# Moving the gated activations of the expert value stage by 64 and 128 bytes within SBUF

## The reference, cut to what matters

```python
def _peer(h, w_q, sub_keys, u_emb, v_emb):
    ...
    def retrieve(args):
        tb, eb, gb = args
        act = jax.nn.gelu(jnp.einsum('tkd,td->tk', u_emb[eb], tb), approximate=False) * gb
        return jnp.einsum('tk,tkd->td', act, v_emb[eb])
...
        x = x + _peer(_rmsnorm(x, norm2_g[l]), peer_w_q[l], peer_sub_keys[l], peer_u[l], peer_v[l])
    return _rmsnorm(x, final_g)
```

## The kernel before, in words

| stage, matmul line | moving operand | stationary operand | stationary minus moving, modulo 256 |
|---|---|---|---|
| value stage, L3329 | `v_gated` 64 | `gated_gelu` 64 | 0 |
| `u_mid`, L3073 | `tok` 64 | `u_mid` 64 | 0 |
| `u_early`, L266 | `tok` 64 | `u_early` 224 | 160 |
| `merged`, L2763 | `merged` 64 | `project_ahead` 160 | 96 |
| gate and up, L503 | `x_hi` 128, `x_lo` 192, plus 64 for each step of k | `w_hi` 64, `w_lo` 0 | 0, 64, 128 and 192 in turn |
| down, L503 | `hidden_hi` 192, `hidden_lo` 64, plus 64 for each step of k | `w_hi` 64, `w_lo` 0 | 0, 64, 128 and 192 in turn |

## Time and profile before

### The profile page before, as it was taken

The page is one execution under the profiler, slowest core; times in us unless marked ns, Lnnn a source line. Parts: engine busy times, 40 slices in busy tenths (PEclk is TensorE's granted clock), DMA queues, the critical chain, the costliest instruction groups (busy, mean ns, idle before and its releaser), DMA issues. The chain is left out here.

```text
span 2236.2 us, 46147 instructions
## 1 busy us (share of the span) xinstructions
PE 2201.7 (98%) x18208; PEld 2091.5 (94%) x18208; DVE 1625.6 (73%) x3097; ACT 1042.5 (47%) x1695; POOL 107.6 (5%) x46
## 2 busy tenths in 40 slices
PE   9999999999999999999899999999999999999998
PEld 9999989999999998999889999999999999888887
DVE  6665868765875687875686587798889966777776
ACT  5444555444544466544453355444444444333333
POOL 0000000000000000000000000188000000000000
PEclk9999999999999999999999999999999999999999
DMA  6553635553555443555332235454444445555554
GB/s 218 175 202 119 210 107 172 176 196 129 185 178 195 155 151 114 181 195 201 119 110 67 78 116 177 167 176 167 151 138 139 140 164 189 192 188 190 192 191 150
DMA packets 100061, 361.11 MB, mean 161 GB/s; under 512 B 11544, under 2 KB 15784, under 8 KB 99760
## 3 DMA queue, kind: packets, MB, share of 16 engines
q1 hardware_dynamic: 99888, 358.65, 47.8%
HBM read 357.55 MB, written 1.05 MB: 160 GB/s over the span
## 5 line engine op out<-in xcount | busy, mean ns | idle before, releaser
L1123 DVE TENSOR_TENSOR w_lo<-ring,w_hi 128x1024 fp32r<-128x1024 f32 (+1 forms) x301 | 393.1, 1308 | 190.8 <-ACT w_hi L872 190.3
L872 ACT ACTIVATE w_hi<-ring 128x1024 fp32r<-128x1024 f32 (+1 forms) x301 | 337.4, 1125 | 344.8 <-PE ps L503 332.4
L503 PE MATMUL ps<-x_hi,w_hi 128*128 128x272 f32 (+1 forms) x1608 | 464.1, 289 | 1.4 <-DVE x_lo L1193 0.9
L503 PE MATMUL ps<-x_hi,w_lo 128*128 128x272 f32 (+1 forms) x1608 | 459.7, 286 | 0.0
L503 PE MATMUL ps<-x_lo,w_hi 128*128 128x272 f32 (+1 forms) x1608 | 458.9, 285 | 0.0
L503 PEld LDWEIGHTS ps<-x_hi,w_hi 128*128 128x128 f32 x1608 | 302.8, 188 | 4.2 <-DVE w_lo L1123 1.5
L503 PEld LDWEIGHTS ps<-x_lo,w_hi 128*128 128x128 f32 x1608 | 302.8, 188 | 0.2
L503 PEld LDWEIGHTS ps<-x_hi,w_lo 128*128 128x128 f32 x1608 | 302.5, 188 | 0.0
L3282 ACT ACTIVATE v_gated_hi<-ring 128x1024 fp32r<-128x1024 f32 x128 | 135.8, 1061 | 213.8 <-PE ps L3329 213.8
L3073 PE MATMUL ps<-tok_hi,u_mid_hi 128*128 128x256 f32 x704 | 204.5, 291 | 0.8 <-POOL u_mid_lo L249 0.8
L3329 PE MATMUL ps<-v_gated_hi,gated_gelu_hi 128*128 128x512 f32 x512 | 201.9, 394 | 0.0
(11 more groups left out here) (522 smaller groups left out, 5081.8 us busy)
## 6 DMA issues: line engine op xcount, KB each, us to landing
ring<-in_gate_up SPq DMA_DIRECT2D x173, 512.0 KB, 3.3
ring<-in_peer_v SPq DMA_DIRECT2D x128, 512.0 KB, 3.2
ring<-in_down SPq DMA_DIRECT2D x64, 704.0 KB, 4.1
ring<-in_peer_u_mid SPq DMA_DIRECT2D x88, 512.0 KB, 3.3
ring<-in_w_in SPq DMA_DIRECT2D x46, 512.0 KB, 3.3
ring<-in_peer_u_early SPq DMA_DIRECT2D x40, 512.0 KB, 3.2
ring<-in_project SPq DMA_DIRECT2D x32, 512.0 KB, 3.8
ring<-in_da_qk SPq DMA_DIRECT2D x18, 512.0 KB, 4.4
```

The costliest lines, as they stand in the source:

```text
L503: mm = nc.tensor.matmul(ps[:, bank, 0:ntok], parts[left][:, slot, t * P:(t + 1) * P], rhs[right][:, k, 0:ntok], start=start and n == 0, st ...
L872: A.activation(parts[0][:, n % SLOTS, 0:width[n]], ring[:, n % SLOTS, 0:width[n]], ACT.Copy).then_inc(hi_done.sem, 1)
L1123: V.tensor_tensor(parts[1][:, n % SLOTS, 0:width[n]], ring[:, n % SLOTS, 0:width[n]], parts[0][:, n % SLOTS, 0:width[n]].bitcast(F32), ALU ...
```

## The change

The two `gated_gelu` tensors get a row pitch of 272 elements (1088 bytes) in place of 256 (1024 bytes), and a small unused tensor is placed ahead of each: 64 bytes before `gated_gelu_hi`, 128 bytes before `gated_gelu_lo`. The start addresses of `gated_gelu_hi` and `gated_gelu_lo` become 128 modulo 256 for buffer 0 and 192 for buffer 1, where all four were 64. The rows of `gate_map` and of `v_gated` stay at 64, so that buffer 0 begins 64 bytes and buffer 1 begins 128 bytes past them. The instructions that write and read the tensors take the first 256 elements of a row, as before. No other tensor that the value stage uses moves, since these are the last ones allocated. The number, the shapes and the order of the instructions are the same on every engine, and so are their waits. Only line numbers shift by four.

```diff
-            gated_gelu = [sb_in(c, f"gated_gelu_{part}", [P, 2, SEQ], F32R) for part in ("hi", "lo")]
+            gelu_pitch = SEQ + 16
+            gated_gelu = []
+            for part in ("hi", "lo"):
+                sb_in(c, f"before_gelu_{part}", [P, 16 if part == "hi" else 32])
+                gated_gelu.append(sb_in(c, f"gated_gelu_{part}", [P, 2, gelu_pitch], F32R))
...
-                    V.tensor_copy(gated_gelu[0][:, b, :], value).then_inc(early_hi.sem, 1)
+                    V.tensor_copy(gated_gelu[0][:, b, 0:SEQ], value).then_inc(early_hi.sem, 1)
                     dve.wait_ge(early_hi.sem, j + 1)
-                    V.tensor_tensor(gated_gelu[1][:, b, :], value, gated_gelu[0][:, b, :].bitcast(F32), ALU.subtract).then_inc(early_lo.sem, 1)
+                    V.tensor_tensor(gated_gelu[1][:, b, 0:SEQ], value, gated_gelu[0][:, b, 0:SEQ].bitcast(F32), ALU.subtract).then_inc(early_lo.sem, 1)
```

## The result

The changed kernel takes 2242.6 us in the median of 17 runs (2241.93 to 2243.86), the kernel before 2238.77 us in 17 runs beside it. The ratio is 1.0018, with a 95% interval of 1.0012 to 1.0025. It became 3.8 us slower. The forecast was 3.7 us faster, and the measured time lies above the range.

The account below looks back on a forecast made before the run. TensorE was taken to bound the kernel, in the value stage by a loop of 3.22 us plus ten even intervals. Saving 58 ns in each of 63 loops gave 3.7 us, from 2238.39 to 2234.7 us, range 2232.8 to 2238.5.

Parts of the forecast that it names:

- The loop of 3.22 us plus ten even intervals: Value stage: four latencies through ScalarE, VectorE and the weight load plus ten even-item matmul intervals make the 5.52 us pair time.
- The cause, the offset between load and stream: TensorE: the matmul pace depends on where the two operands lie, by 2 to 3 ns a matmul.
- no change: Rival: the pace depends on something else that differs between the stages, so the time stays 2238.4 us; chance 0.11.
- I take that for offset 64: 213.3 + 10.4 = 223.7 ns: Value stage, buffer 0: a 512-column matmul at offset 64 costs 10.4 ns over its columns, taken from 256-column stages.
- The unevenness goes: Even items: the uneven intervals after a late weight load, 230 ns on average, become even at 223 to 225 ns.
- The odd items: Value stage, offset 128: they stay hidden up to 231 ns an interval, so they neither give nor take anything.
- The rival "slower": Rival: each buffer 0 interval costs 0.24 us, adding 6.6 us, to 2245.0; it decides from 229.5 ns upward; chance 0.05.
- the mixed stages: Stages `x` and `hidden`, a quarter of pairs at offset 64: faster than the offset 0 stage, held against the slower rival.
- VectorE, ScalarE and the stages ahead: VectorE's and ScalarE's effects were taken as 0, and all stages ahead should keep their times.
- The wait of the weight load for `v_gated_lo`: TensorE in the value stage: this wait should grow from 8.8 us, since TensorE arrives earlier in both kinds of items.
- The signs of being wrong: Value stage: even items keep 227 ns or more, odd items slow to over 231 ns, or the 3.22 us move.

Follow-up runs that it names:

- b0_64_b1_0: Kernel after the change with other paddings, so that buffer 0 has offset 64 and buffer 1 offset 0: 2240.67 us, 1.001 of the kernel before.
- hi_first: Kernel before, with TensorE waiting for `v_gated_lo` only ahead of the last four matmuls of an item: 2234.33 us, 0.9983 of the kernel before.
- both_moved: Kernel before, with `gated_gelu` and `v_gated` both moved to 64 bytes past the value rows, offset 0 between them: 2238.55 us, 1.0002 of the kernel before.
- v_moved: Kernel before, with only `v_gated` moved, so that `gated_gelu` lies 64 bytes past it in both buffers: 2243.64 us, 1.0024 of the kernel before.
- u_mid_moved: Kernel before, with the 256-column stage's weights `u_mid` moved from offset 0 to 64 and 128: 2231.01 us, 0.9969 of the kernel before.
- columns_256: Kernel after, with buffers at offsets 0 and 64 and each value-stage matmul split into two of 256 columns: 2250.13 us, 1.0053 of the kernel before.

## Why the prediction was wrong, point by point

- **The loop of 3.22 us plus ten even intervals: right.** b0_64_b1_0 gave it to 1 ns in 5.56 us, and hi_first, which takes the loop away, brought the steady pace at once. In the pair shown after the change the latencies are 3.25 us in place of 3.22, for the step from the load to the second matmul (0.37).
- **The cause, the offset between load and stream: right.** both_moved and v_moved settle it. The rule of the Trainium skill in "TensorE: Matmul & The Clock Gate", section "Step-by-step: what each phase is for", that the two read ports are independent, gave "no change". The runs differ from it in both directions, by -3.5 ns with 256 columns (-6.7 at offset 64 alone, u_mid_moved) and +6.6 ns with 512.
- **The price, "I take that for offset 64: 213.3 + 10.4 = 223.7 ns": the step that failed.** It carried the cost over the columns from matmuls of 256 columns to those of 512, as if it were a constant of the offset. At offset 64 it is 20.0 ns at 512 columns (233.3 - 213.3), where the prediction had 10.4, and 11.1 ns at 256 columns in columns_256. At offset 0 it is 13.3 at both widths (120.0 and 226.7 ns). It is no constant at one width either: in `u_mid` offset 64 costs 6.6 ns. So of the 5.8 ns that each even interval was to gain, nothing came, and each lost 3.9 instead.
- **"The unevenness goes": wrong where it counts.** At offset 0 the intervals do fall back to a steady 227 ns after a late load. At 512 columns only offset 0 was seen to have such a pace. Moved apart, the intervals spread less in even items (nearly all are 229 to 236 ns, where they were 224 to 238) and more in odd ones (228 to 241, where they were 224 to 236), but around 233 ns. That two streams fall back into step is an interpretation still.
- **The odd items: the bound was right, the value not.** The prediction let them be hidden up to 231 ns, by a sum with 223.7 for the even ones. They came to 232.7, the even ones to 233.3, and TensorE's own 24 intervals, 5.59 us, caught up with the loop, which with even intervals of 233.3 would be 3.22 + 2.33 = 5.56. Against the 5.518 us of before that is 63 x 0.073 = 4.6 us, as in the profiled execution.
- **The rival "slower" had the right threshold and place**, 229.5 ns in buffer 0, at a chance of 0.05, and too high a price (240 ns, 6.6 us). With the measured 233.3 ns its own sum gives 10 x 3.8 x 63 = 2.4 us, which is about what b0_64_b1_0 lost; the other half of the loss came with the odd items, which no rival had. The reason given against it, the mixed stages, was again the one of 256 columns.
- **VectorE, ScalarE and the stages ahead: right**, unchanged to the ns. The wait of the weight load for `v_gated_lo` was to grow. It shrank, by 43 ns in even items (133 to 90), since TensorE arrives later and not earlier.
- **The signs of being wrong** both came: even items over 227 ns and odd ones over 231. Of the two readings given for the first, "offset was not the cause" is ruled out by v_moved, and "64 is no good offset" is right at 512 columns.

That the loss comes from the offset is shown, and so is that its sign differs between 256 and 512 columns. Why it does is open. Whether it is decisive that the weight load ends within an interval was tried at 384 and 448 columns, and neither run bears it out or settles what does.

## What to carry to other kernels

A price read at one width of matmul is no constant that can be added at another, even within one kernel and one engine. Take it from rows of the same width and the same kind of operands, or measure it with two buffers at two offsets in one run, where even and odd items stand side by side. Then look at every part of an item before you average or pick: at 384 columns one token block says the opposite of the other. A wait that is gone from a list may only have fallen below what the list shows; look at the start times. Before a padding is put in for alignment, write down the distances of all operands that are read together: in the pairs that matter here, a shift against one neighbour undid an even distance to another. And a rare, short wait at the head of an item can be the visible end of a loop that is closed all round; moving that wait behind work that does not need it was worth more than any offset in the value stage.

## What the hardware showed that was not expected

- With a weight load for each float32r matmul, stationary and moving operand at the same address modulo 256, the steady start-to-start time is the columns at 2.4 GHz plus 13.3 ns: 120.0 ns at 256 and 226.7 ns at 512 columns, and 173.3 at 384 in one of the two token blocks. It repeats to 1 ns (hi_first), and after a late load it takes up to ten matmuls to come back, at 224 to 240 ns each.
- At any other offset tried there is no such plain steady time at 512 columns: 232.7 to 234.1 ns for 32, 64, 96, 128 and 160, and 229.8 for 192.
- The same 64 is the faster one at 256 columns, by 2.2 ns with activations as the stationary operand (columns_256) and by 6.7 ns in `u_mid`, where the ring item is. Offset 128 gives 1.0 to 1.6 ns there.
